# Attention scores of the second block's mixer: three rounded products of halves in place of one plain f32 product

## The chip, the cores and the metric

The kernel runs as one program on one core of a Trainium2 chip. What is compared is the device time of an execution in microseconds (us), the median of a few runs. The engines of the core are TensorE (PE in the profile, with its weight loads as PEld), VectorE (DVE), ScalarE (ACT), GpSimd (POOL) and SyncE (SP); each works through its own list of instructions in order, and semaphores tie them together.

## The reference, cut to what matters

The reference is two networks one after the other. The first has two layers with windowed attention and retention; the second has two layers, each with three mixers side by side (a long convolution done by Fourier transforms, a differential attention, a pooling), an output projection, a mixture of experts and layer norms. The change touches only the differential attention of the second network, which is done once in each of its two layers, on 512 tokens with 4 heads of 2 x 64 columns:

```python
def diff_attention(q, k, v, ...):            # 4 heads, each with two halves c of 64 columns
    q = apply_partial_rope(q, cos, sin) * (ATT_HEAD_DIM ** -0.5)
    k = apply_partial_rope(k, cos, sin)
    s = einsum('bqhcd,bkhcd->bhcqk', qblk, k)          # for each block of 128 queries
    pr = softmax(s, axis=-1)
    a = pr[:, :, 0] - lam * pr[:, :, 1]
    o = einsum('bhqk,bkhe->bqhe', a, v)
    return rms_norm_2(o, subln_g) * (1.0 - lam_init)
```

So each head and block of queries needs two sums of scores, c = 0 and c = 1, each over 64 columns of q and k.

## The kernel before, in words

Everything is f32. The large projections are done in rounded products: ACT copies an operand to a rounded type (fp32r in the profile), GpSimd subtracts that from the operand, which gives the low half, and PE adds up three products: high by high, low by high and high by low (helper `three`). Such a product is one MATMUL instruction. The scores of the differential attention are plain f32 matmuls instead; each of those stands in the trace as two MATMUL instructions with a weight load each.

The mixer of a layer runs in five functions, one for each engine's list: `pe_mix` (line 2207), `act_mix`, `dve_mix`, `pool_mix`, and SP's list of loads. q and k of head h are `q2[:, h, :]` and `k2[:, h, :]`, 128 partitions (two halves of 64) by 512 tokens. They are made by a projection on PE (`("qk", i, m)`; m is 0 to 3 for q of head m and 4 to 7 for k of head m - 4), a copy of the bank by ACT (`act_rot`), a shuffle by DVE (`dve_rot`), and two multiplications and an addition by GpSimd (`pool_rot`). m = 0, 4, 1, 5, 2 and 6 are projected before the attention's loop; 3 and 7 inside it ("late heads", `QK_AT = {0: 3, 3: 7}`).

The loop has 18 steps `it` (`pe_attention2`, line 2330, and the loops of the same 18 steps in the other engines' lists). Step `it` below 16 is head `it // 4`, block `it % 4`:

- PE does the two score sums of the step into two of the banks 4 to 7. The q of half c stands in rows 64 c to 64 c + 63 of the array, so the two sums use different halves of the array's rows. Each sum waits for ACT's exponential of two steps before in the same half.
- DVE takes the maxima of both banks (L138), ACT the two exponentials with their sums (XF<-PS,SM), DVE the reciprocals (L132). One step later GpSimd scales the second half by the reciprocal and lambda (L123, event `p1`), and another step later DVE mixes both (`mix`, RTX<-XF,SM L126).
- From `it` = 6 on PE transposes four mixed blocks at a time (L108), ACT copies them out, and PE multiplies by v.
- Beside this, the same loop carries the convolution: PE transforms forward (`pe_forward`, RAW operands) at `it` = 1, 2, 4 and 5, DVE and GpSimd multiply spectra (`dve_term`, `pool_term`, at `it` = 4 to 9 and 10 to 15 on GpSimd; DVE's `dve_middle` at `it` = 11), and PE transforms back from `it` = 17 on (`pe_back`), which waits for GpSimd's last term.
- At `it` = 13 and 17 the outputs of heads 0 and 1 are split: ACT writes the rounded half to `Y2.hi` (`act_put`) and GpSimd the rest to `Y2.lo` (`pool_put`).

The order within each list is written out by hand. All elementwise instructions go through helpers, so in the profile L105 is every matmul, L108 a transpose, L114 an ACT activation, L120 a tensor_tensor (DVE or GpSimd), L123 a tensor_scalar, L126 a scalar_tensor_tensor, L132 a reciprocal, L138 a maximum, L147 a shuffle. BF holds q2 and k2, RT and RTX are two names of one memory that holds `Y2`, the spectra and the mixed blocks.

Of the kernel before, what the change touches and what calls it, by code (L numbers as in the profile page):

```python
# [233 lines left out]
def build(nc, io, out):  # L234
    ctx = ExitStack()
    with ctx:
# [1928 lines left out]
        q2 = BF[:, 6824:8872].rearrange("p (a t) -> p a t", a=4)  # L2165
        k2 = BF[:, 8872:10920].rearrange("p (a t) -> p a t", a=4)
        vv = BF[:, 10920:12968].rearrange("p (a t) -> p a t", a=4)
        WIN = BF[:, 6824:8872].rearrange("p (a t) -> p a t", a=4)
        ZT = BF[0:33, 8872:9384]
        fws = BF[0:33, 9384:9448], BF[0:64, 9448:9512]  # L2170
# [9 lines left out]
        rn, la, subg = SM[:, 488:490], SM[:, 490:494], SM[:, 494:495]  # L2180
        nlam = la[:, 3:4]
        nm2, ss2, rs2 = (SM[:, 496 + 4 * k:500 + 4 * k] for k in range(3))
        vn, vs, MID = SM[0:1, 512:1024], BF[0:1, 2056:2568], RTX[0:1, 13312:13824]


        HID = [(scr(0)[0:64, :], scr(1)[0:64, :]), (scr(2)[0:64, :], scr(3)[0:64, :])]
# [147 lines left out]
        def pe_attention2(pe, i):  # L2334


            def first(*banks):
                for n in range(bank.n - 8, bank.n):
                    for count in bank.back.get(n, ()) if n % 8 in banks else ():
                        pe.wait_ge(*count)  # L2340

            for it in range(18):
                if it < 16:
                    h, blk = it // 4, it % 4
                    if it < 2:
                        first(4 + 2 * it, 5 + 2 * it)
                    for c in range(2):
                        pe.wait_ge(*pool_done.at(("qk", i, h)))
                        pe.wait_ge(*pool_done.at(("qk", i, 4 + h)))
                        if it >= 2:  # L2350
                            pe.wait_ge(*act_done.at(("exp2", i, it - 2, c)))
                        pe.matmul(PS[:, 4 + (2 * it + c) % 4, :], q2[64 * c:64 * c + 64, h, blk * P:blk * P + P],
                                  k2[64 * c:64 * c + 64, h, :], True, True).then_inc(*pe_done.done(("s2", i, it, c)))
                for h, j in turned_at(it):
                    pe_turn2(pe, i, h, j)
                if it == 0:
                    first(0)
                    pe_alternate(pe, i)
                if it == 1:
                    first(1, 2, 3)  # L2360
                if it in QK_AT:
                    pe_late_head(pe, i, QK_AT[it])
                for n in FORWARD_AT.get(it, ()):
                    pe_forward(pe, i, n)
                if it == 17:
                    pe_back(pe, i, 0)
                    pe_back(pe, i, 1)
                for h, j in valued_at(it):
                    pe_value2(pe, i, h, j)
                if it in (11, 15):  # L2370
                    pe_mean2(pe, i, (it - 11) // 4)
            pe_value2(pe, i, 2, 3)
            pe_back(pe, i, 2)
            pe_turn2(pe, i, 3, 0)
            pe_turn2(pe, i, 3, 1)
            pe_back(pe, i, 3)
            pe_value2(pe, i, 3, 0)
            pe_mean2(pe, i, 2)
            pe_turn2(pe, i, 3, 2)
            pe_value2(pe, i, 3, 1)  # L2380
            pe_turn2(pe, i, 3, 3)
            pe_value2(pe, i, 3, 2)
            pe_value2(pe, i, 3, 3)
            pe_mean2(pe, i, 3)
            pe.wait_ge(*act_done.at(("oln", i, 3)))
            pe.wait_ge(*dve_done.at(("hread", i, 1)))

        def turn_bank(h, j):
            return PS[:, 7 if h == 3 and j % 2 else 1, :]
# [35 lines left out]
        def act_mix(act, i):  # L2425
# [28 lines left out]
            for c in range(2):  # L2454
                for k in range(4):
                    o = bank.of(("vkT", i, c, k))[:, 0:P]
                    act.wait_ge(*pe_done.at(("vkT", i, c, k)))
                    act.activation(VK[:, k, 0, c * P:c * P + P], o, ACT.Copy).then_inc(*act_done.done())
                    act.activation(VK[:, k, 1, c * P:c * P + P], o, ACT.Copy).then_inc(*act_done.done(("vk", i)))
                    bank.give(("vkT", i, c, k), act_done.now())  # L2460
            for m in (1, 5):
                act_rot(act, i, m, bank.of(("qk", i, m, 0)))
                bank.give(("qk", i, m, 0), act_done.now())
# [4 lines left out]
            for m in (2, 6):  # L2468
                act_rot(act, i, m, bank.of(("qk", i, m, 0)), unit_of(f"wqk{i}", 0))
                bank.give(("qk", i, m, 0), act_done.now())  # L2470
            for it in range(18):
                for h, j in turned_at(it):
                    act_turned(act, i, h, j)
# [4 lines left out]
                if it < 16:  # L2478
                    for c in range(2):
                        q = 2 * (it % 2) + c  # L2480
                        if it >= 3:
                            act.wait_ge(*dve_done.at(("mix", i, it - 3)))
                        act.wait_ge(*dve_done.at(("nm2", i, it)))
                        act.activation(PB[(2 * it + c) % 6], PS[:, 4 + (2 * it + c) % 4, :], ACT.Exp, bias=nm2[:, q:q + 1],
                                       accum_out=ss2[:, q:q + 1]).then_inc(*act_done.done(("exp2", i, it, c)))
                if it in QK_AT:
                    act_rot(act, i, QK_AT[it], PS[:, 0, :])
                for n in FORWARD_AT.get(it, ()):
# [2 lines left out]
                    act_output(act, i, (it - 10) // 4)  # L2491
                if it in (11, 15):
                    act_mean(act, i, (it - 11) // 4)
                if it in (13, 17):
                    h = (it - 13) // 4
                    act_put(act, i, 2 + h, ON[h], dve_done.at(("y", i, 2 + h)))
            act_output(act, i, 2)
            act_turned(act, i, 3, 0)
            act_turned(act, i, 3, 1)
# [73 lines left out]
        def dve_mix(dve, i):  # L2573
# [50 lines left out]
                dve_pooled(dve, i, c)  # L2624
            for m in (1, 5):
                dve_rot(dve, i, m)

            for z in range(2):
                dve.tensor_tensor_reduce(SM[:, 1028:1092], lq[:, 128 * z:128 * z + 64], lq[:, 128 * z + 64:128 * z + 128],
# [9 lines left out]

            for m in (2, 6):  # L2640
                dve_rot(dve, i, m)
            for it in range(18):
                if it < 16:
                    q, z = 2 * (it % 2), 4 + 2 * (it % 2)
# [16 lines left out]
                if 2 <= it <= 17:  # L2661
                    n, q = it - 2, 2 * (it % 2)
                    dve.wait_ge(*pool_done.at(("p1", i, n)))
                    if n >= 8:
                        dve.wait_ge(*pe_done.at(("aT", i, n // 4 - 2, 3)))
                    dve.scalar_tensor_tensor(AR[n % 8], PB[2 * n % 6], rs2[:, q:q + 1], PB[(2 * n + 1) % 6], ALU.mult, ALU.add
                                             ).then_inc(*dve_done.done(("mix", i, n)))
                if it - 1 in QK_AT:
                    dve_rot(dve, i, QK_AT[it - 1])
                if it in (12, 16):  # L2670
# [181 lines left out]
        def pool_mix(pool, i):  # L2852
# [21 lines left out]
                    lo_upto(pool, ("vt2", i, half, tl))  # L2874
            for m in (1, 5):
                pool_rot(pool, i, m)
            for c in range(2):
                pool_put(pool, i, 6 + c, POOLED[c][2])
            for m in (2, 6):
                pool_rot(pool, i, m, unit_of(f"wqk{i}", 0))  # L2880
            for it in range(18):
                if 1 <= it <= 16:
                    n, q = it - 1, 2 * ((it - 1) % 2) + 1
                    p = PB[(2 * n + 1) % 6]
                    pool.wait_ge(*dve_done.at(("rs2", i, n)))
                    pool.tensor_scalar(p, p, rs2[:, q:q + 1], nlam, ALU.mult, ALU.mult).then_inc(*pool_done.done(("p1", i, n)))
                if it - 1 in QK_AT:
                    pool_rot(pool, i, QK_AT[it - 1])
                if it in MERGED_AT:
                    pool_term(pool, i, *MERGED_AT[it])  # L2890
                if it in (13, 17):
                    h = (it - 13) // 4
                    pool_put(pool, i, 2 + h, ON[h])
            lo_upto(pool, ("back", i, 2), unit_of(f"wout{i}", 0))
            for c in range(2):
                pool_put(pool, i, c, HYO[c])
# [1019 lines left out]
```

## Time and profile before

| what | us |
|---|---|
| median of 3 runs | 3111.28 (3110.03 to 3116.8) |
| span of the profiled execution | 3111.6 |
| attention loop and backward transform, layer 1 | about 2119.6 to 2223.6 |
| the same, layer 2 | about 2680.6 to 2782.7 |
| PE busy in the span | 2924.9 (94%) |

Times in the trace are counted from the start of the span. The profile gives no time outside of the span; the span and the median of the runs are 0.3 us apart. A timeline line reads: start, duration, engine, source line, operation, tiles written and read, shape, number of merged instructions, and in brackets how long the engine stood idle before it and for whom. Durations of matmuls contain a modelled end, so the distance between two starts says more than a duration.

### The profile page before, as it was taken

Reading aid. Unit: us, or ns where it says so; the run is one execution under the profiler, and the core shown is the slowest. Engines: PE = TensorE matmul, PEld = TensorE weight load, DVE = VectorE, ACT = ScalarE, POOL = GpSimd, SP = SyncE. Lnnn points to the kernel's source line nnn. Section 1 sums busy time; section 2 is a strip of 40 time slices with the busy share of each in tenths; the row PEclk is TensorE's granted clock in tenths of the full one; section 3 lists DMA queues with packets and bytes.
Section 4 is the critical chain, followed back from the end, with each engine's and each line's share of the span. In section 5 each row is a group of like instructions: output and inputs, shape, how many; then the busy total and the mean of one; then the engine's idle time right before and its main releaser. Section 6 shows DMA issues by size and latency. Waiting matters only on the chain.

```text
span 3111.6 us, 40118 instructions
## 1 busy us (share of the span) xinstructions
PE 2924.9 (94%) x15552; PEld 2152.9 (69%) x15552; DVE 1480.0 (48%) x2252; ACT 1179.5 (38%) x1847; POOL 1314.0 (42%) x798
## 2 busy tenths in 40 slices
PE   7999989999999999999999999999889889979997
PEld 4666657888888788888978888685564237646533
DVE  5665545562331544443351111555575555456665
ACT  5334425122111423333242222424544653464465
POOL 3644333454443444353435554448531024763200
PEclk9999999999999999999999999999999989999998
DMA  5310213444332112121123233221247942114795
GB/s 228 109 35 14 75 68 122 143 148 149 122 109 67 49 55 75 48 88 54 62 93 102 95 95 102 68 69 47 69 183 311 401 153 82 55 50 182 263 382 202
DMA packets 85885, 375.13 MB, mean 121 GB/s; under 512 B 9408, under 2 KB 11968, under 8 KB 76608
## 3 DMA queue, kind: packets, MB, share of 16 engines
q1 hardware_dynamic: 68416, 310.41, 28.5%
q10 hardware_dynamic: 12672, 45.37, 3.7%
q0 software_dynamic: 4608, 16.78, 1.5%
q8 instruction: 125, 2.05, 0.3%
q14 instruction: 64, 0.52, 0.1%
HBM read 557.07 MB, written 29.36 MB: 188 GB/s over the span
## 4 chain that ended last, share of the span: by engine, by line
PE 77%; DVE 10%; ACT 4%; DMA 3%; POOL 3%; issue 2%; SPq 0%; DVEq 0%; POOLq 0%; ACTq 0%
PE PS L105 76%; DVE SCR L120 2%; DMA ALL<-in_moe 2%; PE PS L108 1%; POOL RTX L120 1%; ACT SCR L114 1%; DMA BF<-in_ada 1%; DVE SCR L126 1%; DVE XF L126 1%; DVE SM L120 1%; ACT RT L114 1%; DVE SCR L132 1%; ACT WH L114 1%; DVE BF L132 1%; POOL XF L123 1%
## 5 line engine op out<-in xcount | busy, mean ns | idle before, releaser
L105 PE MATMUL PS<-RT,WH 128*128 128x512 f32 (+1 forms) x5696 | 1515.1, 368 | 32.2 <-ACT SCR L114 10.2
L105 PEld LDWEIGHTS PS<-RT,WH 128*128 128x128 f32 x5696 | 1028.2, 190 | 266.8 <-issue 30.4
L120 POOL TENSOR_TENSOR WL<-RAW,WH 128x1024 fp32r<-128x1024 f32 x284 | 701.4, 2472 | 776.8 <-ACT WH L114 776.6
L105 PE MATMUL PS<-RT,WL 128*128 128x512 f32 (+1 forms) x2848 | 924.5, 366 | 0.0
L105 PEld LDWEIGHTS PS<-RT,WL 128*128 128x128 f32 x2848 | 492.2, 191 | 56.6
L114 ACT ACTIVATE WH<-RAW 128x1024 fp32r<-128x1024 f32 x284 | 298.6, 1055 | 600.4 <-PE PS L105 542.2
L120 POOL TENSOR_TENSOR RT<-SCR,RT 128x512 fp32r<-128x512 f32 (+2 forms) x174 | 222.4, 1284 | 403.5 <-ACT RT L114 309.3
L105 PE MATMUL PS<-ALL,SCR 128*32 x576 | 267.0, 607 | 24.6 <-DVE SCR L120 14.0
L120 DVE TENSOR_TENSOR SCR<-PS,SCR 128x512 f32<-128x512 f32 (+1 forms) x106 | 58.9, 572 | 485.8 <-PE PS L105 468.7
L105 PE MATMUL PS<-RTX,SCR 128*32 128x512 f32 x1152 | 267.2, 613 | 0.0
L126 DVE SCALAR_TENSOR_TENSOR XF<-PS,SM,XF 128x512 f32<-128x512 f32 x240 | 149.7, 658 | 216.8 <-PE PS L105 216.2
L114 ACT ACTIVATE SCR<-PS 128x512 f32<-128x512 f32 (+1 forms) x272 | 137.7, 526 | 245.4 <-PE PS L105 226.9
L114 ACT ACTIVATE RT<-SCR 128x512 fp32r<-128x512 f32 (+2 forms) x130 | 72.1, 572 | 345.5 <-DVE SCR L120 342.2
L117 DVE COPY RTX<-ALL 128x1024 f32 x216 | 142.7, 691 | 115.1 <-PE PS L105 92.7
L105 PEld LDWEIGHTS PS<-ALL,SCR 128*32 128x32 f32 x576 | 58.0, 111 | 190.3 <-issue 187.8
L156 POOL DMA_INDIRECT BF<-placed_out,PLACE x12 | 11.3, 946 | 361.4 <-DMA placed_out<-RTX 358.3
L105 PE MATMUL PS<-WH,RT 128*128 128x256 f32 x864 | 161.8, 283 | 0.0
L105 PE MATMUL PS<-BF 128*128 128x512 f32 (+2 forms) x324 | 139.1, 634 | 10.9 <-DVE SCR L120 4.4
L105 PEld LDWEIGHTS PS<-WH,RT 128*128 128x128 f32 x864 | 137.4, 192 | 0.5
L105 PE MATMUL PS<-RAW,SCR 128*32 128x512 f32 x576 | 137.2, 597 | 0.0
L129 DVE CUSTOM_DVE_ANT_0 SCR<-BF 128x1024 f32<-128x1024 f32 x64 | 118.3, 1876 | 30.7 <-DMA BF<-in_ada 28.2
L120 DVE TENSOR_TENSOR SCR<-SCR 128x512 f32<-128x512 f32 x100 | 89.1, 891 | 88.7 <-ACT SCR L114 82.5
(239 smaller groups left out, 3637.7 us busy)
## 6 DMA issues: line engine op xcount, KB each, us to landing
ALL<-in_moe SPq DMA_DIRECT2D x100, 2048.0 KB, 9.0
ALL<-in_moe SPq DMA_DIRECT2D x100, 1024.0 KB, 14.0
RAW<-in_ff SPq DMA_DIRECT2D x132, 512.0 KB, 3.6
BF<-in_ada SPq DMA_DIRECT2D x64, 512.0 KB, 4.8
RAW<-in_ret SPq DMA_DIRECT2D x64, 512.0 KB, 3.6
RAW<-in_win SPq DMA_DIRECT2D x28, 512.0 KB, 3.6
RTX<-in_ada SPq DMA_DIRECT2D x26, 512.0 KB, 5.1
XF<-placed_in ACTq DMA_DIRECT2D x24, 512.0 KB, 8.8
```

Of the source, the lines that this page charges most:

```text
L105: return NOTHING if self.e is None else self.e.matmul(o, w, x, start=first, stop=last)
L108: return NOTHING if self.e is None else self.e.transpose(o, x, ident)
L114: return NOTHING if self.e is None else self.e.activation(*a, **k)
L117: return NOTHING if self.e is None else self.e.tensor_copy(*a)
L120: return NOTHING if self.e is None else self.e.tensor_tensor(*a)
L123: return NOTHING if self.e is None else self.e.tensor_scalar(*a)
L126: return NOTHING if self.e is None else self.e.scalar_tensor_tensor(*a)
L129: return NOTHING if self.e is None else self.e.tensor_tensor_reduce(*a)
L132: return NOTHING if self.e is None else self.e.reciprocal(o, x)
L156: return NOTHING if self.e is None else self.e.indirect_dma_start(*a)
```

## The change

The scores become three rounded products for each sum. For head m the high half of q and k is copied by ACT into two buffers in the memory of `Y2` (tiles 2 and 3, high and low); the low half is the difference, written in place over q2 and k2: by GpSimd for q, by DVE for k. Two heads' high halves fit at a time, so heads 2 and 3 are split inside the loop, at `it` = 5 and 8, after the scores of head 0 or 1 are done. PE does all three products of sum c = 0 and then all three of c = 1; the wait for the exponentials is one for both sums, on the later of the two. Since the buffers lie in tiles 2 and 3 of `Y2`, the outputs of heads 0 and 1 are put there only at `it` = 16 and 17, not at 13 and 17. A one-row scratch (`MID`) moves out of the buffers' way.

```diff
@@ names @@
+        QK2R = BFR[:, 6824:10920].rearrange("p (a t) -> p a t", a=8)
+        QK2H = [RT[:, 9216:10240], RT[:, 13312:14336]]
+        QK2HF = [RTF[:, 9216:10240], RTF[:, 13312:14336]]
-        vn, vs, MID = SM[0:1, 512:1024], BF[0:1, 2056:2568], RTX[0:1, 13312:13824]
+        vn, vs, MID = SM[0:1, 512:1024], BF[0:1, 2056:2568], BF[0:1, 1024:1536]
@@ pe_attention2 @@
-                    for c in range(2):
-                        pe.wait_ge(*pool_done.at(("qk", i, h)))
-                        pe.wait_ge(*pool_done.at(("qk", i, 4 + h)))
-                        if it >= 2:
-                            pe.wait_ge(*act_done.at(("exp2", i, it - 2, c)))
-                        pe.matmul(PS[:, 4 + (2 * it + c) % 4, :], q2[64 * c:64 * c + 64, h, blk * P:blk * P + P],
-                                  k2[64 * c:64 * c + 64, h, :], True, True).then_inc(*pe_done.done(("s2", i, it, c)))
+                    pe_scores2(pe, i, it)
@@ new functions @@
+        def pe_scores2(pe, i, it):
+            h, blk = it // 4, it % 4
+            pe.wait_ge(*act_done.at(("qh", i, h)))
+            pe.wait_ge(*act_done.at(("qh", i, 4 + h)))
+            pe.wait_ge(*pool_done.at(("ql", i, h)))
+            pe.wait_ge(*dve_done.at(("ql", i, 4 + h)))
+            if it >= 2:
+                pe.wait_ge(*act_done.at(("exp2", i, it - 2, 1)))
+            q, k = ((split_high(m)[0], QK2R[:, m, :]) for m in (h, 4 + h))
+            for c in range(2):
+                r = slice(64 * c, 64 * c + 64)
+                for n, (a, b) in enumerate(((0, 0), (1, 0), (0, 1))):
+                    t = pe.matmul(PS[:, 4 + (2 * it + c) % 4, :], q[a][r, blk * P:blk * P + P], k[b][r, :], n == 0, n == 2)
+                    if n == 2:
+                        t.then_inc(*pe_done.done(("s2", i, it, c)))
+        def act_split(act, i, m):
+            act.wait_ge(*pool_done.at(("qk", i, m)))
+            if m % 4 >= 2:
+                act.wait_ge(*pe_done.at(("s2", i, 4 * (m % 4) - 5, 1)))
+            act.activation(split_high(m)[0], (q2 if m < 4 else k2)[:, m % 4, :], ACT.Copy).then_inc(*act_done.done(("qh", i, m)))
+        def eng_split(eng, done, i, m):
+            eng.wait_ge(*pool_done.at(("qk", i, m)))
+            eng.wait_ge(*act_done.at(("qh", i, m)))
+            eng.tensor_tensor(QK2R[:, m, :], (q2 if m < 4 else k2)[:, m % 4, :], split_high(m)[1], ALU.subtract).then_inc(
+                *done.done(("ql", i, m)))
+        SPLIT_AT = {5: 2, 8: 3}
@@ act_mix: after the copies of vkT; after rot 2 and 6; in the loop @@
+            for m in (0, 4):
+                act_split(act, i, m)
...
+            for m in (1, 5):
+                act_split(act, i, m)
...
+                if it in SPLIT_AT:                      # after the exponentials of the step
+                    for m in (SPLIT_AT[it], 4 + SPLIT_AT[it]):
+                        act_split(act, i, m)
...
-                if it in (13, 17):
-                    h = (it - 13) // 4
-                    act_put(act, i, 2 + h, ON[h], dve_done.at(("y", i, 2 + h)))
+                if it >= 16:
+                    h = it - 16
+                    act_put(act, i, 2 + h, ON[h], dve_done.at(("y", i, 2 + h)), pe_done.at(("s2", i, 15, 1)))
@@ dve_mix: after rot 5; after rot 6; in the loop, after the mix of the step @@
+            eng_split(dve, dve_done, i, 4)
...
+            eng_split(dve, dve_done, i, 5)
...
+                if it in SPLIT_AT:
+                    eng_split(dve, dve_done, i, 4 + SPLIT_AT[it])
@@ pool_mix: after rot 5; after rot 6; in the loop, after p1 of the step @@
+            eng_split(pool, pool_done, i, 0)
...
+            eng_split(pool, pool_done, i, 1)
...
+                if it in SPLIT_AT:
+                    eng_split(pool, pool_done, i, SPLIT_AT[it])
...
-                if it in (13, 17):
-                    h = (it - 13) // 4
-                    pool_put(pool, i, 2 + h, ON[h])
+                if it >= 16:
+                    pool_put(pool, i, it - 14, ON[it - 16])
```

## Rows read from the trace of the kernel before

**Rows 1.** Windows of layer 1: stretch, length, busy time by engine, clock, DMA.
```profile
2119.60:2147.00 27.40, 26.04 (x93) 13.79 (x94) 10.35 (x15) 11.27 (x25) 16.89 (x13) 1.00 0.12 39
2157.00:2177.00 20.00, 16.77 (x51) 6.62 (x50) 18.43 (x24) 12.10 (x31) 19.28 (x19) 0.83 0.05 20
```
**Rows 2.** The chain that ended last, layer 1: start, us, what.
```profile
2123.91 22.97 PE PS L105 x80
...
2150.19 2.50 POOL SCR L120 x2
...
2176.77 0.69 DVE VLX L120
...
2191.61 1.23 POOL RT L120
```
**Rows 3.** Timeline of PE, layer 1: start, us, what, idle before and for whom.
```profile
2119.66 2.94 PE L105 MATMUL PS<-BF 64*128 64x512 f32 x12 [0.78 <-ACT SCR L114]
...
2134.27 1.13 PE L105 MATMUL PS<-BF 64*128 64x512 f32 x4
2135.33 3.70 PE L105 MATMUL PS<-BF,RAW 128*128 128x512 f32 x8
...
2159.23 1.13 PE L105 MATMUL PS<-BF 64*128 64x512 f32 x4
...
2200.14 5.39 PE L105 MATMUL PS<-RAW,RTX 128*128 128x256 f32 x16 [0.69 <-POOL RTX L120]
```
**Rows 4.** The same timeline cut at 2134.5, and cut at 2165.5.
```profile
2134.27 0.70 PE L105 MATMUL PS<-BF 64*128 64x512 f32 x2
...
2165.23 0.69 PE L105 MATMUL PS<-BF 64*128 64x512 f32 x1 [0.27 <-ACT XF L114]
```
**Rows 5.** Timeline of PE: rounded products, full rows, then half rows.
```profile
2127.22 0.39 PE L105 MATMUL PS<-RT,WL 128*128 128x512 f32 x1
2127.45 0.62 PE L105 MATMUL PS<-RT,WH 128*128 128x512 f32 x2
2127.90 0.39 PE L105 MATMUL PS<-RT,WL 128*128 128x512 f32 x1
...
113.07 0.56 PE L105 MATMUL PS<-BFR,RT 64*128 64x256 f32 x4
113.56 0.45 PE L105 MATMUL PS<-VL,IDR 128*128 128x384 f32 x1
```
**Rows 6.** Timeline of GpSimd (POOL), layer 1.
```profile
2116.94 2.52 POOL L120 TENSOR_TENSOR RT<-SCR,RT 128x512 fp32r<-128x512 f32 x2
...
2132.18 0.77 POOL L123 TENSOR_SCALAR XF<-XF,SM 128x512 f32<-128x512 f32 x1 [5.07 <-DVE SM L132]
...
2156.27 0.76 POOL L123 TENSOR_SCALAR XF<-XF,SM 128x512 f32<-128x512 f32 x1
...
2158.43 1.71 POOL L123 TENSOR_SCALAR XF<-XF,SM 128x512 f32<-128x512 f32 x1
```
**Rows 7.** Timeline of DVE, layer 1.
```profile
2152.80 1.76 DVE L120 TENSOR_TENSOR VLX<-VLX 128x512 f32<-128x512 f32 x1
...
2156.28 1.23 DVE L138 TENSOR_REDUCE SM<-PS 128x2 f32<-128x1024 f32 x1 [0.58 <-PE PS L105]
```
**Rows 8.** Timeline of ACT, layer 1.
```profile
2118.92 0.60 ACT L114 ACTIVATE SCR<-PS 128x512 f32<-128x512 f32 x1 [4.84 <-PE PS L105]
2122.66 0.59 ACT L114 ACTIVATE SM<-PS 1x512 f32<-1x512 f32 x1 [3.13 <-PE PS L105]
...
2207.35 0.60 ACT L114 ACTIVATE SCR<-PS 128x512 f32<-128x512 f32 x1 [6.69 <-PE PS L105]
```
**Rows 9.** Timeline of PE, layer 2.
```profile
2751.16 2.08 PE L105 MATMUL PS<-BF 64*128 64x512 f32 x4
...
2760.56 0.66 PE L108 MATMUL PS<-IDT,RTX 128*128 128x128 f32 x4 [0.91 <-ACT SCR L114]
2761.05 3.62 PE L105 MATMUL PS<-RAW,RTX 128*128 128x256 f32 x16
```

More of the change, by code:

```diff
@@ L2386, in pe_attention2, with split_high @@
             pe.wait_ge(*dve_done.at(("hread", i, 1)))
+        def split_high(m):
+            c = 512 * (m // 4)
+            return QK2H[m % 2][:, c:c + 512], QK2HF[m % 2][:, c:c + 512]
+        def pe_scores2(pe, i, it):
[24 more added lines that the diff above has]
+        SPLIT_AT = {5: 2, 8: 3}
         def turn_bank(h, j):
```

## The prediction

> **What bounds the kernel now.** I first cut layer 1's loop into stretches with the windows view [rows 1], then read the chain of waits through it [rows 2], then each engine's timeline there. The whole kernel is PE's, but the loop is not. From 2119.6 to 2147 PE is busy for 26.0 of 27.4 us; the chain runs on PE without a break from 2123.9 to 2146.9. From 2157 to 2177 PE is busy for 16.8 of 20 us while GpSimd is busy for 19.3 and DVE for 18.4, and the chain is GpSimd's: from 2150.19 it goes from one GpSimd instruction to the next, until DVE takes it over at 2176.77 (a term and the middle row), and back over GpSimd to the backward transform, which PE starts at 2200.14 after 0.69 us of waiting for GpSimd [rows 3]. The reader is to see that there are two regimes: up to step 4 what PE does counts; from step 4 to step 11 what GpSimd does counts, and PE's matmuls there are free. Layer 2 has the same pattern 561 us later, except that its backward transform begins behind a transpose that waited for ACT, not behind GpSimd [rows 9].
>
> **Part 1, the scores themselves.** There are 16 pairs of sums in each layer. A pair now takes 1.06 us of PE, from start to start of what follows [rows 3]. The two sums of a pair lie in different rows of the array and run together: each streams 512 columns four times, 0.853 us at 2.4 GHz, and the other 0.21 us is the weight load at the front and the change back to full rows. Had the sums run one after the other the pair would have taken over 1.7 us. Rounded products of half rows overlap too: two groups of 256 + 384 columns take 0.49 us [rows 5], which is 0.27 us of streaming for one group and the same 0.22 us on top; both groups in series would be 0.53 us of streaming alone. In the stream of full rows a rounded product of 512 columns takes 0.68 / 3 = 0.227 us (2127.22 to 2127.90) [rows 5].
>
> With three products for each sum, what matters is whether sum 1's first product starts beside sum 0's first, or has to wait until sum 0's third has started, as the order in the list would have it. Overlapped: 3 x 0.213 + 0.21 + 0.02 of gaps = 0.87 us, 0.19 less than now. In strict order sum 1 starts beside the third product, five streams in all: 5 x 0.227 + 0.21 = about 1.33 us, 0.27 more than now. With no overlap whatever, 6 x 0.227 + 0.21 = 1.57 us. The trace speaks for the first. A plain f32 sum is itself two matmul instructions (four for a pair, rows 3). Cut at 2134.5 the timeline shows two of the four started; at 2165.23, where the second sum still waits for its exponential, the same cut (0.27 us on) shows only one [rows 4]. So at 2134 the two that had started are one of each sum: sum 1's first half went ahead of sum 0's second. If the halves are issued sum by sum, PE does not keep the list's order between different rows of the array. I cannot see the order of issue, so this is evidence and no proof. I take 0.87 us.
>
> The Trainium skill speaks against this: "TensorE: Matmul & The Clock Gate", Part 3 (packing small matmuls), says that matmuls keep program order in start and end, without reordering. By that rule the pair would come out longer than before, not shorter; the trace's two early starts [rows 4] agree with the rule only if an f32 product's two halves are not issued one after the other.
>
> On the path are the pairs of steps 0 to 4 (the chain's PE stretch and the pair before it): 5 x -0.19 = **-0.95 us** in each layer. Those of steps 5 to 14 lie beside GpSimd and give nothing. Step 15's lies on PE's way to the backward transform: -0.19 in layer 1, and -0.37 in layer 2, where it runs at 1.2 GHz, 2.08 us long instead of the 1.13 of the others [rows 9, 3]. The joint wait for the later exponential moves sum 0's start by at most one exponential (0.6 us) and only where PE has slack.
>
> **Part 2, the splits.** Each layer gains 8 ACT copies, 4 GpSimd subtractions and 4 DVE subtractions of 128x512. GpSimd's cost 2.52 / 2 = 1.26 us with 0.07 of issue, about 1.33 (the same form of instruction: rounded out, two f32 in) [rows 6]. An ACT copy of this size is 0.6 us. A DVE instruction with two inputs in SBUF took 1.76 us beside a busy GpSimd [rows 7]; the chain's DVE piece took 0.69 [rows 2].
>
> Heads 0 and 1, before the loop: ACT's copies for head 0 fall in a wait for PE; those for head 1 come behind the copy at 2118.92 and end about 2120.8, and ACT's next work is at 2122.66 after 3.13 us idle [rows 8]. GpSimd's subtraction for head 0 stands behind its rotation of m = 5, which ends just before 2116.94, so it ends at about 2118.3; the first scores start at 2119.66 [rows 3], so 1.3 us are left. The two puts and the rotations behind it move back by 1.33 and 2.67 us, but GpSimd then idled for 5.07 us [rows 6]. I cost all this at nothing; if that cover is thin, the first scores wait, up to 1 us.
>
> Heads 2 and 3, at steps 5 and 8: both of GpSimd's subtractions fall into the stretch where GpSimd is the chain: 2 x 1.33 = **+2.67 us**. Nothing hides them. DVE's two run beside. DVE has 0.58 us idle at step 6 [rows 7], and it too is nearly full (18.4 of 20 us). With ACT's two copies ahead of it at step 8 it stalls for up to 1 us, so DVE comes out 2 us later, just under GpSimd, which stays last. But both engines also lengthen each other: the same tensor_scalar of GpSimd took 0.76 us at one place and 1.71 at another where DVE was at a two-input instruction [rows 6]. Two more DVE instructions of 0.7 us cost GpSimd between 0 and 0.95 us each; I take half of 0.7 each, **+0.7 us** for each layer (bounds 0 and 1.9). Scores of step 8 need GpSimd's first subtraction, ready at about 2158; they started at 2159.23 [rows 3], so this wait does not show.
>
> **Part 3, the moved puts.** GpSimd's subtraction at step 13, 1.23 us on the chain (the last line) [rows 2] and 1.26 with its share of issue, goes behind the last term, so GpSimd's way to the backward transform gets **-1.26 us**. The two puts at steps 16 and 17 then end near 2205; ACT, which needs head 0's put out of its buffer, reads head 2's output at 2207.35 after 6.69 us idle for PE [rows 8], so they are hidden. ACT's put at 13 was not on the chain. MID's move costs nothing: same instructions.
>
> **The sum.** At step 11, each layer: -0.95 + 2.67 + 0.7 = +2.4. Layer 1: GpSimd's way ends at +2.4 - 1.26 = +1.2; PE's and ACT's way through mixes, transposes and scores 15 ends at +2.4 - 0.2 = +2.2, and had 0.69 us of slack: +1.5. The later is +1.5. Layer 2 has no such slack: +2.4 - 0.37 = +2.0. Together **+3.6 us**. The profiled span of 3111.6 becomes 3115.2. The median stands 0.3 below that span: **3114.9 us**.
>
> **Rivals.**
>
> A. Strict order on PE (a pair at 1.33 us), the rule quoted above taken as a mechanism of this kernel: each pair on the path is 0.46 worse than in my sum; 5 pairs in each layer, and step 15 with 0.46 and 0.9: +6.0 on top, 3120.9 us. For it: a list is worked through in order on every other engine here, and the halves of an f32 product may be issued otherwise than I assume. Against: rows 4. This is the one that ends slower: the place is PE from 2119.6 to 2147, and the change turns slower by over 0.2% as soon as a pair takes more than about 1.27 us. 15%.
>
> B. The splits are absorbed. If GpSimd's stretch gives way (fewer collisions with DVE, instructions falling into each other's gaps), the gains are left: layer 1 -1.8 (PE's and ACT's way: -0.95 - 0.19 - 0.69), layer 2 -1.3: 3108.2 us. For it: some of GpSimd's instructions are stretched to twice their length there, so that there is time to be had. Against: GpSimd 19.3 of 20 us busy. 15%.
>
> C. The clock. It is 0.83 from 2157 to 2177 [rows 1]; the first 16 matmuls of the backward transform took 5.39 us in layer 1 and 3.62 in layer 2 [rows 3, 9]. With less for PE to do in the loop, both layers could run this stretch at 1.2 GHz (+2 to +4 us, 3118), or both at 2.4 (-1.8, 3113). 15% for the slower of these.
>
> D. DVE takes GpSimd's place: stalled by ACT's copies at step 8 and stretched by GpSimd, it comes out 1.5 us later than GpSimd in each layer: 3118 us. 10%.
>
> My own case has 45%, with a range of 3112 to 3118. The measurement tells about 0.2% from no change, 6.2 us: 3105.1 to 3117.5. Slower than that are A, and a part of C, D and of my own: 23%. Faster is the far end of B: 10%. The range for 8 of 10 is 3108 to 3121.
>
> **What would show it.** The trace after has 6 matmuls of 64x512 for a pair; from the first start to what follows it should be 0.87 us, and a cut 0.3 us in should show two started. 1.3 us would be rival A. PE's stretch to step 4 should be 1 us shorter, GpSimd should show two more subtractions BFR between 2155 and 2170 with no new idle time around them, and the backward transforms should start 1.5 and 2 us later, counted from the first scores. If these start earlier than before, my reading that GpSimd's stretch has no slack is wrong; if the first scores wait for GpSimd, part 2's cover was.

## The result and the profile after

The changed kernel takes 3121.29 us in the median of 15 runs (3115.48 to 3127.08), the kernel before 3113.11 in 15 runs beside it (3105.52 to 3118.18). The ratio is 1.0026, with a 95% interval of 1.0017 to 1.0034: +8.2 us, between 5.3 and 10.6. So the change is slower, by a quarter of a percent. I had forecast 3114.9, +3.6 over the 3111.28 that were shown. The sign was right and the size was too small: the median lies 0.3 us above the top of my range. 1.8 us of the miss are the base, whose median with more runs is 3113.11. The 0.3 us that I took off the span belongs to it: wherever the record has the span and the time of one execution, the time is the longer by 1.75 us or more (3118.93 against 3117.1 for the profile below), so a span of 3111.6 goes with a time of about 3113.4.

The profiled spans are 3111.6 and 3117.1. The page of the changed kernel, sections 1 and 4: PE has lost 16 us of busy time, the others have gained, and PE's share of the chain fell from 77% to 74% while DVE's rose from 10% to 12%.

```profile
PE 2908.9 (93%) x15616; PEld 2154.6 (69%) x15616; DVE 1499.5 (48%) x2260; ACT 1188.2 (38%) x1863; POOL 1327.8 (43%) x806
...
PE 74%; DVE 12%; ACT 4%; DMA 4%; POOL 3%; issue 3%; SPq 1%; DVEq 0%; POOLq 0%; ACTq 0%
```

**The pair of sums** is what I forecast. PE's timeline, as in [rows 3] and [rows 4]:

```profile
2134.90 0.50 PE L105 MATMUL PS<-RT 64*128 64x512 f32 x2
2135.24 0.39 PE L105 MATMUL PS<-RT,BFR 64*128 64x512 f32 x2
2135.47 0.39 PE L105 MATMUL PS<-BFR,RT 64*128 64x512 f32 x2
2135.80 3.70 PE L105 MATMUL PS<-BF,RAW 128*128 128x512 f32 x8
```

The list has three products of sum 0 and then three of sum 1, but the timeline merges them two and two by operand: both high-by-high products run first, together, then both low-by-high, then both high-by-low. From the first start to the transform behind it are 0.90 us (predicted 0.87) against 1.06.

**The stretch of GpSimd** is where the time goes. GpSimd's timeline around the two new subtractions, to be held against [rows 6]:

```profile
2156.87 0.76 POOL L123 TENSOR_SCALAR XF<-XF,SM 128x512 f32<-128x512 f32 x1
2157.60 1.70 POOL L120 TENSOR_TENSOR BFR<-BF,RT 128x512 fp32r<-128x512 f32 x1
2159.44 1.54 POOL L120 TENSOR_TENSOR RTX<-RTX,VLX 128x512 f32<-128x512 f32 x1
2160.97 1.29 POOL L123 TENSOR_SCALAR XF<-XF,SM 128x512 f32<-128x512 f32 x1
...
2170.08 1.69 POOL L120 TENSOR_TENSOR BFR<-BF,RT 128x512 fp32r<-128x512 f32 x1
```

The two BFR lines are the new subtractions, with no idle time about them. They take 1.70 and 1.69 us, where I had taken 1.26 from [rows 6]. DVE then waits for GpSimd at the term of step 11, which came at 2176.77 before [rows 2]:

```profile
2180.54 0.75 DVE VLX L120
...
2192.10 0.48 PE PS L108
2192.57 3.29 PE PS L105 x8
2195.87 1.06 PE PS L108 x4
```

These are lines of the chain of waits (start, us, what). The last three are on PE's way to the backward transform: a transpose, the value product with pair 15, and the next transposes. They run at 1.2 GHz, see below. The transform itself starts here:

```profile
2203.36 0.65 PE L108 MATMUL PS<-IDT,RTX 128*128 128x128 f32 x4 [0.91 <-ACT SCR L114]
2203.85 3.62 PE L105 MATMUL PS<-RAW,RTX 128*128 128x256 f32 x16
```

It waits for transposes that waited for ACT, as layer 2 did before [rows 9], and no longer for GpSimd [rows 3].

**One table for all kernels.** I count each loop from the start of its first scores to four marks: the forward transform of step 4 (end of PE's stretch), the first row product of DVE's middle (step 11, end of GpSimd's stretch), the backward transform, and the first product of the output projection behind it. Layer 1 / layer 2, in us, from the profiled execution of each kernel:

```
kernel          step 4          step 11         backward        projection
before          27.09 / 27.09   57.71 / 57.78   80.48 / 80.36   103.92 / 102.03
changed         26.29 / 26.28   60.59 / 60.59   83.24 / 83.24   104.92 / 104.91
c_after         26.29 / 26.29   60.54 / 60.63   82.53 / 83.27   104.20 / 104.95
e_products      26.31 / 26.29   57.05 / 57.03   79.69 / 79.69   101.36 / 101.36
e_splits        27.13 / 27.13   61.01 / 61.02   82.89 / 83.28   105.04 / 104.95
e_gpsimd_only   26.30 / 26.29   59.16 / 59.22   81.80 / 81.84   103.47 / 103.51
e_dve_only      26.28 / 26.29   57.71 / 57.71   80.10 / 79.60   101.76 / 101.27
e_early         26.28 / 26.30   58.76 / 58.76   80.88 / 81.24   102.55 / 102.90
e_early_dve     26.32 / 26.30   58.01 / 57.98   80.23 / 80.71   101.91 / 102.38
e_two_heads     26.31 / 26.27   56.97 / 56.94   79.71 / 79.68   103.28 / 103.11
e_alternate     26.26 / 26.28   60.53 / 60.54   83.15 / 83.15   104.83 / 104.82
e_apart         31.27 / 31.37   65.54 / 65.98   86.99 / 87.42   108.66 / 109.09
e_short_late    26.28 / 26.28   60.36 / 60.50   82.13 / 82.28   103.80 / 103.95
e_puts          27.11 / 27.10   57.89 / 57.89   79.95 / 80.32   101.62 / 101.99
```

In most kernels the first two columns repeat within 0.1 us between layers and executions, and the third within 0.75. That is far finer than the timed medians, whose single runs spread over 12 us or more. Up to the backward transform the changed kernel's loops are 2.76 and 2.88 us longer, 5.6 us together.

The last column says what of this is left, and in layer 1 it is less. The first 16 matmuls of the backward transform took 5.39 us there before, at 1.2 GHz [rows 3]. They take 3.62 in the changed kernel (the line at 2203.85), so 1.8 us come back behind the mark. At the projection the changed kernel is 1.0 us later in layer 1 and 2.9 in layer 2: 3.9 us in place of 5.6. "Loops" below means the third column.

Seven of the experiments (e_gpsimd_only, e_dve_only, e_alternate, e_apart, e_early, e_short_late, e_puts) were timed once each, 3105.7 to 3126.6 us. I use these runs for their marks alone.

### The profile page after: what moved, and what is told of

It is laid out like the page before. It is cut to its first block, busy times and chain, and to the rows that moved or that the text cites. A ratio compares the mean times of both kernels' runs of the same rounds, so it can differ in the third digit from the quotient of the medians.

```text
span 3117.1 us, 40277 instructions
## 1 busy us (share of the span) xinstructions
PE 2908.9 (93%) x15616; PEld 2154.6 (69%) x15616; DVE 1499.5 (48%) x2260; ACT 1188.2 (38%) x1863; POOL 1327.8 (43%) x806
## 4 chain that ended last, share of the span: by engine, by line
PE 74%; DVE 12%; ACT 4%; DMA 4%; POOL 3%; issue 3%; SPq 1%; DVEq 0%; POOLq 0%; ACTq 0%
PE PS L105 73%; DVE SCR L120 2%; DMA ALL<-in_moe 2%; PE PS L108 1%; DVE XF L126 1%; DMA BF<-in_ada 1%; DVE SCR L126 1%; DVE SM L120 1%; ACT SCR L114 1%; ACT RT L114 1%; POOL RTX L120 1%; DVE XF L120 1%; DVE SCR L132 1%; DVE BF L132 1%; ACT WH L114 1%
## 5 line engine op out<-in xcount | busy, mean ns | idle before, releaser
L114 ACT ACTIVATE BF<-PS 128x512 f32<-128x512 f32 (+3 forms) x208 | 91.4, 482 | 105.1 <-PE PS L105 103.5
```

The lines of the kernel that those rows point to most:

```text
L114: return NOTHING if self.e is None else self.e.activation(*a, **k)
```

## The experiments

**e_products: no splits inside the loop.**

```diff
-                if it in SPLIT_AT:      # the three uses, in ACT's, DVE's and GpSimd's list
...
+            h = h % 2                   # in pe_scores2
```

> The changed kernel without the six splits inside each loop (ACT, GpSimd and DVE at steps 5 and 8); the scores of heads 2 and 3 are computed from the halves of heads 0 and 1, so those heads' values are left out. The puts stay at steps 16 and 17. I measure a loop from the start of its first scores to the start of its backward transform: before 80.5 us in layer 1 (2119.66 to 2200.14), after 83.2 (2120.61 to 2203.85). Theory 1 (the loss is the in-loop splits on GpSimd's stretch, the products themselves gain 0.16 us a pair for 5 pairs): 79.4 to 79.8 us for each loop, and the kernel's time 1 to 3 us under before, about 6 to 10 under the changed one. Rival 1 (the loss of the changed kernel is not in the loops, since its median is 8.2 us up and the two loops only 5.7): the time stays 3 us or more above before though the loops are short. Rival 2 (the joint wait and the products' own waits cost): loops stay above 81.

Loops 79.69 us, step 11 at 57.05: as theory 1 says. So the products, with the late puts, make each loop 0.7 to 0.8 us shorter than before. The splits inside the loop (four copies of ACT, two subtractions each of GpSimd and DVE) cost 60.59 - 57.05 = 3.5 us up to step 11. The time, 3125.64 us (ratio 1.0038, 1.0024 to 1.0052), went the other way, and I do not use it: with other attention values the tokens go to other experts, and the span outside the two loops is 2917 us here against 2899 to 2912 in all others. That the routing is the cause was not tested.

**e_splits: all splits, plain f32 scores.**

```diff
-            eng.tensor_tensor(QK2R[:, m, :], (q2 if ...
+            eng.tensor_tensor(split_high(m)[0], (q2 if ...
-                for n, (a, b) in enumerate(((0, 0), (1, 0), (0, 1))):
-                    t = pe.matmul(...)
+                pe.matmul(PS[:, 4 + (2 * it + c) % 4, :], q2[r, h, ...], k2[r, h, :], True, True)...
```

> The changed kernel with plain f32 scores: all splits and the late puts stay, the low halves are written over the high ones, and PE reads q2 and k2 themselves. Theory 1: loops 0.8 to 1.0 us longer than in the changed kernel, about 84.1 us, and the time about 2 us above the changed kernel, 10 above before. Rival 1: the time is as before plus 3 or less above the changed one's loop gain, that is no simple sum. Rival 2: loops shorter than the changed kernel's 83.2.

Step 4 is back at 27.13, 0.84 us later than in the changed kernel: that is the products' whole gain, 5 pairs. At step 11 half of it is left (61.01 against 60.59), and at the backward transform nothing clear (82.9 and 83.3 against 83.24). I expected 84.1; the gain on PE does not pass through to the end in full. In layer 1 pair 15 ran at 2.4 GHz here, 1.06 us from 2193.10 to 2194.16, and the leg from step 11 to the backward transform took 21.88 us against 22.65 in the changed kernel. The ratio to before is 1.0046 (1.0030 to 1.0062, 7 runs), in the expected direction, but the medians are 11.9 us apart and the loops 5.3: the rest is not explained.

**e_gpsimd_only and e_dve_only: one engine's in-loop subtractions.**

```diff
-                    eng_split(dve, dve_done, i, 4 + SPLIT_AT[it])     # e_gpsimd_only
...
-                    eng_split(pool, pool_done, i, SPLIT_AT[it])       # e_dve_only
```

> The changed kernel without DVE's two subtractions inside each loop; the k of heads 2 and 3 is taken from heads 0 and 1. Loops: theory 1 (GpSimd's subtractions carry the loss, 1.33 us each when DVE does not collide): 82.0 to 82.6 us against 83.2. Rival (DVE's subtractions carry it): 80 or less.

> The changed kernel without GpSimd's two subtractions inside each loop; the q of heads 2 and 3 is taken from heads 0 and 1. Loops: theory 1: 79.8 to 80.5 us. Rival (DVE's subtractions carry the loss): 82.5 or more.

Each of the two kernels leaves out two subtractions and takes the low half alone from heads 0 and 1; all of ACT's copies stay in. Against 57.05 with no split inside, step 11 comes at 59.16 with GpSimd's two (+2.1), at 57.71 with DVE's two (+0.7), and at 60.59 with both (+3.5, where the sum would be 2.8). The loops (81.8; 80.1 and 79.6) follow. GpSimd carries most of the loss, but DVE's two are worth 1.4 us once GpSimd's are there. What ACT's copies cost by themselves was not measured; it is inside both the 2.1 and the 0.7. The two subtractions in GpSimd's timeline, e_gpsimd_only:

```profile
2153.86 0.78 POOL L123 TENSOR_SCALAR XF<-XF,SM 128x512 f32<-128x512 f32 x1
2154.60 1.27 POOL L120 TENSOR_TENSOR BFR<-BF,RT 128x512 fp32r<-128x512 f32 x1
...
2166.12 1.69 POOL L120 TENSOR_TENSOR BFR<-BF,RT 128x512 fp32r<-128x512 f32 x1
```

The first is 1.27 us, against 1.70 in the changed kernel. The second is 1.69 with no subtraction of DVE in the loop, so it is not DVE's subtractions alone that lengthen GpSimd's. Beside the first it was DVE's product of two inputs that was long, 1.66 us; beside the second DVE's was long too, 1.75:

```profile
2154.76 1.66 DVE L120 TENSOR_TENSOR VLX<-VLX 128x512 f32<-128x512 f32 x1
...
2166.61 1.75 DVE L120 TENSOR_TENSOR VLX<-BF 128x512 f32<-128x512 f32 x1
```

**e_alternate: the order of the products.**

```diff
-            for c in range(2):
-                r = slice(64 * c, 64 * c + 64)
-                for n, (a, b) in enumerate(((0, 0), (1, 0), (0, 1))):
+            for n, (a, b) in enumerate(((0, 0), (1, 0), (0, 1))):
+                for c in range(2):
+                    r = slice(64 * c, 64 * c + 64)
```

> The changed kernel with the products of the two sums in turn (high by high of both, then low by high of both, and so on). The pair takes 0.90 us from start to start in the changed kernel. If PE keeps separate order for different rows of the array: the same 0.90, loops 83.2. If the order in the list costs anything: shorter than 0.90.

The pair takes 0.89 us (2145.66 to 2146.55) and the loops 83.15: no different. The timeline is the same as with one sum ahead of the other:

```profile
2145.66 0.50 PE L105 MATMUL PS<-RT 64*128 64x512 f32 x2
2145.99 0.39 PE L105 MATMUL PS<-RT,BFR 64*128 64x512 f32 x2
2146.23 0.40 PE L105 MATMUL PS<-BFR,RT 64*128 64x512 f32 x2
2146.55 3.70 PE L105 MATMUL PS<-BF,RAW 128*128 128x512 f32 x8
```

**e_apart: no overlap of the two sums.**

```diff
+                if c:
+                    pe.wait_ge(*pe_done.at(("s2", i, it, 0)))
```

> The changed kernel with sum 1 waiting for sum 0's end, so that nothing overlaps. Theory 1: a pair takes 1.6 to 1.8 us where it took 0.90, the five pairs on PE's path cost 3.5 to 4.5 us, loops 86.7 to 87.7. Rival (PE's pairs are not on the path, the loop is GpSimd's throughout): loops under 84.

```profile
2129.78 0.50 PE L105 MATMUL PS<-RT 64*128 64x512 f32 x1
2130.12 0.39 PE L105 MATMUL PS<-RT,BFR 64*128 64x512 f32 x1
2130.35 0.39 PE L105 MATMUL PS<-BFR,RT 64*128 64x512 f32 x1
2130.80 0.49 PE L105 MATMUL PS<-RT 64*128 64x512 f32 x1
2131.13 0.39 PE L105 MATMUL PS<-RT,BFR 64*128 64x512 f32 x1
2131.36 0.38 PE L105 MATMUL PS<-BFR,RT 64*128 64x512 f32 x1
2131.68 1.55 PE L105 MATMUL PS<-BF,RAW 128*128 128x512 f32 x3
```

A pair now takes 1.90 us, 1.0 more, and step 4 comes 5.0 and 5.1 us later: five pairs on the path, one for one. So the count of five and the worth of overlapping are both confirmed. But only 3.8 and 4.2 us arrive at the backward transform, although all 16 pairs are longer. The last leg, step 11 to the transform, is 21.4 us here and 22.65 in the changed kernel.

**e_early: head 2's splits at step 3.**

```diff
-        SPLIT_AT = {5: 2, 8: 3}
+        SPLIT_AT = {3: 2, 8: 3}
```

> The changed kernel with head 2's splits at step 3 instead of 5, head 3's left at step 8. GpSimd's subtraction of head 2 then falls into its idle time, its other one stays in the full stretch. Theory 1: the middle row's start, counted from the first scores, was 60.6 us with both in the stretch, 57.05 with none: 58.6 to 59.1 now, the loops 81.2 to 81.7. Rival (ACT's copies, not the subtractions, delay the stretch): the middle row at 60 or later.

Step 11 at 58.76, loops 80.9 and 81.2. The moved subtraction falls into GpSimd's idle time of step 3 (it stands at 2143.80, and GpSimd still idles 3.23 us before its next instruction). One GpSimd subtraction, with its DVE partner and ACT's two copies, out of the full stretch gives 1.8 us for each layer. The rival of the expectation, ACT's copies, is not told apart by this, since they moved too.

**e_early_dve: no GpSimd split left in the full stretch.**

```diff
+                if it == 11:
+                    eng_split(dve, dve_done, i, 3)       # DVE, ahead of the terms
...
-                    eng_split(pool, pool_done, i, SPLIT_AT[it])
+                if it == 3:
+                    eng_split(pool, pool_done, i, 2)
```

> The changed kernel with the splits of head 2 at step 3, where GpSimd and DVE stand idle, and with head 3's subtraction for q moved from GpSimd at step 8 to DVE at step 11, where DVE waits for GpSimd. No GpSimd split is left in its full stretch. All is computed. Theory 1: loops 79.6 to 80.4 us, time 0 to 3 us under before. Rival 1: time still 3 us or more above before. Rival 2, with DVE as the cause: DVE has one subtraction less in steps 5 to 8 but one more at 11, loops about 81.5.

Loops 80.2 and 80.7, 3112.65 us in 12 runs, ratio 0.9997 (0.9985 to 1.0008): all products are rounded, and the whole timed loss is gone. It is level with before and no faster. DVE's extra subtraction (1.21 us at 2180.48) stands ahead of the term on the path and gives part of it back.

**e_two_heads: products for heads 0 and 1 only.**

```diff
+            if h >= 2:
+                ...                      # the plain f32 sums of before, with their own waits
+                return
```

> Rounded products for heads 0 and 1 alone, which are split ahead of the loop; heads 2 and 3 keep their plain f32 scores and their two waits, and the puts stand at steps 13 and 17 as before. All is computed. Theory 1: only the gain of 5 pairs is left, loops 79.6 to 79.8 us, time 1 to 2 us under before (too small to be told for certain from no change). Rival 1: 3 us or more above before. If the splits ahead of the loop were not hidden, the first scores would start later against the last projection than before.

Loops 79.7, 0.7 us less than before in each layer; 3114.16 us in 12 runs, ratio 0.9999 (0.9987 to 1.0011). The gain of the change where it is worth something, on PE's stretch, is 1.5 us for both layers up to the backward transform. In this execution it is gone at the projection (103.28 and 103.11, together 0.4 us more than before), because the first 16 matmuls of the transform ran at 1.2 GHz in both layers: 5.52 us in layer 1, starting at 2203.97. Neither version beats the kernel before beyond doubt.

**e_puts: the kernel before with the late puts.**

```diff
-                if it in (13, 17):
+                if it >= 16:
```

> The kernel before with the two puts moved to steps 16 and 17, and nothing else. The recorded forecast gives GpSimd's way to the backward transform 1.26 us by this. Theory 1 (the way over ACT and PE ends 0.1 to 0.7 us behind GpSimd's, so it takes over at once): GpSimd's last term ends about 79.0 us after the first scores instead of 80.3 and 80.1, the loops take 79.8 to 80.4. Rival (GpSimd's way was the bound alone): loops 79.2.

GpSimd's last term ends 78.8 us after the first scores, 1.5 and 1.2 us sooner than before (80.33 and 80.06). The loops take 79.95 and 80.32: layer 1 gains 0.53, layer 2 nothing. GpSimd's way frees up and the way over PE and ACT takes over at once.

**e_short_late: one product for each sum from step 5 on.**

```diff
-                for n, (a, b) in enumerate(((0, 0), (1, 0), (0, 1))):
+                for n, (a, b) in enumerate(((0, 0), (1, 0), (0, 1))[:3 if it < 5 else 1]):
```

> The changed kernel with one product in place of three for each sum of steps 5 to 15 (the low halves' products are left out there). This takes some 0.45 us from each of these 11 pairs at full clock and asks what such time is worth. Theory 1 (PE's pairs behind step 4 are not on the path): forward transform of step 4 at 26.3, middle row at 60.4 to 60.6, loops 82.6 to 83.2 us. What the recorded forecast assumed, that step 15's pair is worth its full difference: 82.3 to 82.8. If PE were the bound throughout: 78.5.

Step 11 at 60.36 and 60.50: seven shorter pairs give 0.1 to 0.2 us together, so pairs 5 to 11 are off the path. The loops are 82.1 and 82.3, 1.0 us shorter than the changed kernel's. That is more than theory 1 allowed and a little beyond the 82.3 to 82.8 for a pair 15 that is worth its full difference. The trace tells which pair it is: PE's timeline of pair 15 and the transposes behind it, layer 1:

```profile
2188.82 0.79 PE L105 MATMUL PS<-RT 64*128 64x512 f32 x2
2189.54 1.12 PE L108 MATMUL PS<-IDT,RTX 128*128 128x128 f32 x4
```

The pair takes 0.72 us and not 1.59, and the leg behind step 11 is 21.77 us and not 22.65. So at 1.2 GHz pair 15 alone is worth 0.87 us, and all of it arrives at the transform.

**c_after: the changed kernel again.**

> The changed kernel once more, on another chip or at another time. The loops give +2.8 and +2.9 us against before; the first timing gave +8.2 (5.3 to 10.6). Theory 1 (all of the change's cost is in the two loops, the rest was spread of the measurement): loops 83.2 us again, a ratio of 1.001 to 1.003, that is +3 to +8 us. Rival 1 (a cost outside of the loops): ratio 1.0026 or more again, with the same stretch outside of the loops longer in both profiles.

3119.74 us in 12 runs, ratio 1.0024 (1.0012 to 1.0035), +7.5 us, between 3.7 and 10.9. The loops are 82.53 and 83.27. Its span is 3112.5 against 3117.1 of the first profile of the same kernel, with loops only 0.7 us shorter, so single spans wander by 4 us outside of the loops. The rest of the span (span less both loops up to the output projection) was 2905.7 us before, 2911.9 in e_puts, and 2907.3 and 2903.4 in the two profiles of the changed kernel. In parts: up to layer 1's first scores 2119.7 before, then 2120.6 and 2117.3 in the two profiles of the changed kernel; from projection to the next first scores 457.1, 458.2 and 456.8; from layer 2's projection to the end 328.9, 328.5 and 329.2. No part is longer in both, so rival 1 found no support, but a cost of 2 us there would be lost in this spread.

## Why the prediction was right or wrong

**The scores.** Right. Overlapped pair 0.87 predicted, 0.90 measured; -0.95 for five pairs, -0.80 measured at step 4. Rival A, the strict order, is out: e_alternate is the same as the changed kernel, and e_apart shows what a pair without overlap takes, 1.90 us. The reading of [rows 4] held. The rule that I quoted from "TensorE: Matmul & The Clock Gate", Part 3, of the Trainium skill, that matmuls keep program order in start and end, does not hold here between different rows of the array: sum 1's first product starts in the slot of sum 0's first, in front of sum 0's second and third (2134.90 against 2135.24 and 2135.47).

**The splits ahead of the loop, and the terms of GpSimd's stretch.** Right in kind, a little small in size. The first scores still wait for ACT alone (0.73 us against 0.78 before in layer 1, 0.83 against 0.69 in layer 2). For the two subtractions with their collisions I took 2.67 + 0.7 = 3.4 us; from step 4 to step 11 the loop went from 30.6 to 34.3, +3.7 in layer 1 and +3.6 in layer 2. The split of the sum was off: GpSimd's own two cost 2.1, DVE's 0.7, and 0.8 comes only when both are there (e_gpsimd_only, e_dve_only). DVE did not become the bound (rival D): it idles 1.62 us for GpSimd just before the term of step 11. Rival B is out, since nothing was absorbed. Up to step 11 I had +2.4; it was +2.88 and +2.81, so 0.9 us of the miss in both layers together lie here. GpSimd's own way to the backward transform came out as forecast: its last term ends 0.95 us later than before in layer 1 and 1.25 in layer 2, where I had +1.2.

**The step that failed** is the one behind step 11, where I let the sum shrink again: "ends at +2.4 - 0.2 = +2.2, and had 0.69 us of slack: +1.5" for layer 1 and "+2.4 - 0.37 = +2.0" for layer 2. Measured, the last leg went from 22.77 to 22.65 and from 22.58 to 22.65: -0.12 and +0.07, where I had counted -0.9 and -0.4. That is 1.25 us for both layers. The slack itself was real: e_puts takes 0.53 of it in layer 1. What was mis-sized is the way over PE and ACT. In layer 1 it took 22.77 - 0.69 = 22.08 us before and 22.65 after, +0.57 in place of my -0.2.

The terms, from start to start on PE: I had let pair 15 alone change. In layer 2 it did as I said, from 2.01 to 1.58 us (-0.43, forecast -0.37). But the value product in front of it went from 1.64 to 1.85 and the transposes behind it from 0.49 to 0.91, which I had put at nothing. In layer 1 the value product went from 0.95 to 1.84, and pair 15 did not gain 0.19 but lost 0.53, from 1.06 to 1.59. All of them ran at 1.2 GHz in the changed kernel. The granted clock in two neighbouring stretches of that leg (start to end, length, PE busy, clock, DMA), around pair 15; before, layer 1, then layer 2:

```profile
2182.90:2188.50 5.60, 3.35 (x11) 1.00 0.00 0
2188.50:2194.20 5.70, 4.85 (x15) 1.00 0.02 4
...
2744.00:2749.60 5.60, 3.11 (x11) 1.00 0.00 0
2749.60:2755.30 5.70, 5.70 (x15) 0.70 0.01 3
```

The changed kernel, layer 1:

```profile
2186.90:2192.50 5.60, 1.84 (x11) 0.84 0.00 0
2192.50:2198.20 5.70, 5.70 (x16) 0.55 0.01 1
```

e_apart, layer 1, where PE's pairs are twice as long:

```profile
2190.30:2195.90 5.60, 5.49 (x22) 1.00 0.00 0
2195.90:2201.60 5.70, 4.69 (x16) 1.00 0.01 1
```

In the changed kernel PE works 1.84 of the first 5.6 us where it worked 3.35, and the clock is at 1.2 GHz for the value product, pair 15 and the transposes, all on the path: 1.59 us for the pair in place of 0.90 (2194.21 to 2195.80). In e_apart PE works 5.49, the clock stays at 2.4 GHz, and the leg is 1.2 us shorter although its pairs are longer. That such time is paid one for one is shown by e_short_late, whose pair 15, also at 1.2 GHz, is 0.87 us shorter and whose leg is shorter by as much.

Why the clock falls where it does is not shown. A less busy PE is one reading, and the rows above fit it. Others do not. e_puts in layer 1, with the matmuls of the kernel before, and c_after in layer 1, the changed kernel itself:

```profile
2186.97:2192.49 5.52, 3.27 (x10) 1.00 0.00 0
2192.49:2198.01 5.52, 5.52 (x15) 0.69 0.02 4
...
2183.38:2188.88 5.50, 1.76 (x11) 1.00 0.00 0
2188.88:2194.37 5.49, 5.49 (x17) 0.69 0.00 1
```

With 3.27 us of work the clock falls here, and with 3.35 it did not; with 1.76 it falls no further than with 3.27. The kernel before has its fall too: in layer 2 around pair 15 (0.70 above), in layer 1 a few us later, on the last transposes and the backward transform. c_after's leg in layer 1, 21.99 us, is the shorter one because its value product took 1.31 us and not 1.84; its pair 15 took the same 1.59. So the clock is not a loss that only the changed kernel has. What differs is which matmuls it meets, and for how long. I had it as rival C, with the backward transform as its only place; the second half of that rival, both transforms at 2.4 GHz and -1.8 us, is what happened, while the leg in front of the transform had more of its matmuls at 1.2 GHz. No run changed PE's work in that stretch alone.

**What the sum came to.** Up to the backward transform the two loops gave +5.6 against 3.5 in my sum (+1.5 and +2.0): 0.9 from before step 11, 1.25 from behind it. Up to the projection they gave +3.9. That this lies next to my 3.6 is luck: 2.1 us too much in the loops and 1.8 us back in a transform that I had left unchanged.

**The rest.** The two profiles place 3.9 us (3.2 with c_after), the two timings say +8.2 and +7.5. The first interval starts at 5.3, so something is missing, unless the one profile of the kernel before, with its slow transform in layer 1, stands badly for its runs. What is missing goes with the splits inside the loop, since e_early_dve, timed in 12 runs, loses all of it. The granted clocks of the timed runs point to more time at 1.2 GHz: their mean is 0.9722 in the changed kernel's 15 runs and 0.9725 in c_after's 12, against 0.9752 in the 17 runs of the kernel before that stand beside c_after. Within either kernel a run with a clock lower by 0.001 is 1.4 to 1.9 us longer (a line through c_after's 12 runs and through those 17), so 0.0027 would be about 4 to 5 us. That is an estimate from runs that merely go together, and the profiled pair has it the other way round (0.973 before, 0.975 changed). Where in the span the clock would be lost, and whether it is the cause, stays open.

A slip in the rivals: by the sum as it stands the change turns slower by 0.2% not when a pair takes more than 1.27 us, but from about 1.07 on, since from 3.6 to 6.2 there are 2.6 us and ten pairs, and the two of step 15, carry them.

## What to carry to other kernels

Where an engine's stretch bounds a loop, work that moves from PE to that engine is paid in full, and its partner on an engine that collides with it adds more: here 0.8 us saved cost 3.6. The same subtractions, put into the engine's idle step or onto an engine that waits, gave the same arithmetic at no loss (e_early_dve). A saving on PE behind the bounding stretch should not be booked as time before it is known at which clock the matmuls around it run: pair 15 and its neighbours took up to twice as long at 1.2 GHz.

Cut a loop at marks on two or three engines and compare the legs; that resolved 0.1 us where 15 timed runs resolved 2.6. But put one mark behind everything that the change can move: at the backward transform the loss was 5.6 us, at the projection 3.9.

## What the runs showed of the hardware that I had not expected

Rounded products of two sums in different halves of the array's rows start together, whichever order the list has: 0.90 us for the pair with one sum ahead of the other, 0.89 in turn, 1.90 when a wait keeps them apart.

GpSimd's 128x512 subtraction took 1.27 us in one place, beside a DVE product that took 1.66, and 1.70 in the same place of the changed kernel. The two engines' subtractions together cost 0.8 us more than the sum of each alone (3.5 against 2.1 + 0.7).

With each pair on PE longer by 1.0 us, the leg behind step 11 was shorter by 1.2 us, with the granted clock at 1.00 where it was 0.84 and 0.55.
